# Matrix products that stream their columns by turns, and weight tiles that begin 64 bytes past a multiple of 256

## The chip, the cores and the metric

The kernel runs on one core of a Trainium2 chip, as one launch. The metric is the device time of the launch in microseconds (us): 1811.39 us is the median of 3 runs of the kernel before (1809.56 to 1812.52).

## The reference

Two blocks of layers on one sequence of 512 tokens with 1024 features, all in float32. Nearly all the arithmetic is in matrix products with weights that are read once from HBM:

```python
def reference(x, ...):
    # first block: width 1024, causal convolution of 31 taps, pooling, SwiGLU with 2816 hidden columns
    z = rmsnorm(x, g_mix) @ w_in + b_in
    y = concatenate([conv_group(z[..., :512], z[..., 512:1024]), pool_group(z[..., 1024:])])
    h = x + y @ w_out
    h = h + (silu(rmsnorm(h, g_ffn) @ w_gate) * (rmsnorm(h, g_ffn) @ w_up)) @ w_down
    x = rmsnorm(h, g_final)
    # second block: layer 0 gated causal attention (16 heads), layer 1 differential attention (8 heads)
    for layer in range(2):
        x = layer_norm(ALPHA * x + attention(x), ...)
        u = causal_conv3(x @ ffn_w_in[layer])          # 1024 -> 2 * 2816
        x = layer_norm(ALPHA * x + (silu(u[..., :2816]) * u[..., 2816:]) @ ffn_w_out[layer], ...)
```

## The kernel before

Activations lie with the features over the 128 partitions and the 512 tokens along the free dimension: XH and XL are [128, 8, 512], 2048 bytes for one row k of 128 features. The stationary operand of a product is a 128x128 piece of a weight matrix, the moving operand is such a row of activations (128x512), and the sum over k builds up in one bank of PSUM (bank0, bank1, and in places the banks called attended, score and turned).

TensorE takes float32 in a rounded form, so each operand is split in two: a top part (WH, XH, and HH and OH for the hidden columns and the attention's output) and a low part (WL, XL, HL, OL), the rest. One product is three matmuls, `product` at L982 to L985: WH with XL, WH with XH, WL with XH. Each matmul brings its own load of 128x128 weights (PEld in the profile, over the time of the matmul before).

A weight matrix is worked off in items, pieces of up to 8 rows k by 128 columns. SyncE fetches an item into `raw` (2 places), ScalarE writes its top part into WH (L1605), GpSimd the low part into WL (L742), 4 places each. The order of the items is fixed (the table STAGES). `step` (L987) waits for the halves of the item on w_lo and issues `product`, `item` loops over k, `whole` (L1011) is one item of 8 rows into one bank: 24 matmuls of 512 columns. VectorE or ScalarE reads the finished bank and gives it back over bank_read.

Some products don't run over 512 columns at once: `half_item` (L1036) and `stage_in_halves` (L1048) take 256 columns, so that the norm of one half of the tokens can be made beside the products of the other. `first_items`, `conv_low`, `mixer_items` and `last_rows_of` issue the same three matmuls in another order than `product`, since their operands become ready one row after the other. `conv_pairs` (L1284) runs a quarter of the convolution on TensorE, with diagonal matrices (dg_h, dg_l) as weights and u_h, u_l as moving operand, 256 columns, which begin 4 bytes later from one step m to the next. The two attention stages (qkv1, qkv2) weave: between the products of one pair of heads stand scores, transposes (`turn_map`, L1424) and value products of the pair before. These attention matmuls (`score_packed`, `score`, `attend_folded`, transposes) call pe.matmul directly; only `attend` of the second attention layer uses `product`.

Where the tiles lie in a partition matters for this change: XH, XL, raw, WH, WL, HH, HL, OH, OL, dg_h, dg_l, the value tiles and the identity all begin at a multiple of 256 bytes. u_h and u_l are the exception, since they are shifted. Rows of 2048 bytes and weight pieces of 512 bytes keep that, so in the kernel before the moving operand and the next weights both begin at a multiple of 256 (but for the convolution).

Of the kernel before, what the change touches and what calls it, by code (L numbers as in the profile page):

```python
# [61 lines left out]
RAW = 2  # L62
SLOTS = 4
HALF = S // 2
LAST_DOWN = (3, 3, 8, 8)
assert sum(LAST_DOWN) == FT

# [130 lines left out]
def two_blocks(nc, A, out):  # L198
    ctx = ExitStack()
    with ctx:  # L200
# [19 lines left out]
        yout = sb("yout", [P, 2 * QT, S])  # L220
        last_rows = sb("last_rows", [P, DT, S])
        raw = sb("raw", [P, RAW, DT, P])
        WH = sb("WH", [P, SLOTS, DT, P], F32R)
        WL = sb("WL", [P, SLOTS, DT, P], F32R)
        par = sb("par", [P, 6 * P])
# [2 lines left out]
        ident = identr.bitcast(F32)  # L228
        masks = sb("masks", [P, 2, P], F32R)
        work = sb("work", [P, 6, S])  # L230
        small = sb("small", [P, 108 + 20])

        tmp = [work[:, 0, :], work[:, 1, :]]
        ring = [work[:, i, :] for i in (0, 1, 4, 5)]
# [744 lines left out]

        @block.tensor  # L980
        def _(pe):
            def product(out_, wh, wl, xh, xl, start, stop):  # L982
                pe.matmul(out_, wh, xl, start=start, stop=False)  # L983
                pe.matmul(out_, wh, xh, start=False, stop=False)  # L984
                return pe.matmul(out_, wl, xh, start=False, stop=stop)  # L985

            def step(g, b, hi, lo, k0, k, kt, start, stop, turned=False):  # L987

# [57 lines left out]
            def stage_in_halves(name, m):  # L1046


                g, u = STAGES[name]
                for h in range(2):  # L1050
                    c = slice(h * HALF, (h + 1) * HALF)

                    def by_low(k):
                        pe.wait_ge(x_lo, DT + half_tile(m, h, k) + 1)
                        for j in range(2):
                            mm = pe.matmul(bank[(u + j) % 2][:, c], WH[:, (g + j) % SLOTS, k, :], XL[:, k, c],  # L1056
                                           start=False, stop=k == DT - 1)
                            if h == 1 and k == DT - 1:
                                mm.then_inc(item_done, 1)

                    for k in range(DT):
                        pe.wait_ge(x_top, half_tile(m, h, k) + 1)
                        for j in range(2):
                            if h == 0 and k == 0:
                                bank_free(Nth(u + j))
                                pe.wait_ge(w_lo, 2 * (g + j + 1))
                            s = (g + j) % SLOTS
                            pe.matmul(bank[(u + j) % 2][:, c], WH[:, s, k, :], XH[:, k, c], start=k == 0, stop=False)  # L1068
                            pe.matmul(bank[(u + j) % 2][:, c], WL[:, s, k, :], XH[:, k, c], start=False, stop=False)  # L1069
                        if k:  # L1070
                            by_low(k - 1)
                        if h == 0 and k == 2:
                            whole_sums(m, 1)
                        if h == 0 and k == 3:
                            half_stats(m, 1)
                        if h == 0 and k == 5:
                            half_widen(m, 1)
                    by_low(DT - 1)
# [167 lines left out]
            def first_items():  # L1246

                def by_low(k):
                    pe.wait_ge(x_lo, k + 1)
                    for j in range(2):  # L1250
                        mm = pe.matmul(bank[j][:, :], WH[:, j, k, :], XL[:, k, :], start=False, stop=k == DT - 1)
                        if k == DT - 1:
                            mm.then_inc(item_done, 1)

                for k in range(DT):
                    first_ready(k)
                    pe.wait_ge(x_hi, k + 1)
                    for j in range(2):
# [2 lines left out]
                            pe.wait_ge(w_hi, j + 1)  # L1261
                        elif k == DT // 2:
                            pe.wait_ge(w_lo, j + 3)
                        pe.matmul(bank[j][:, :], WH[:, j, k, :], XH[:, k, :], start=k == 0, stop=False)
                        if k == 0:
                            pe.wait_ge(w_lo, j + 1)
                        pe.matmul(bank[j][:, :], WL[:, j, k, :], XH[:, k, :], start=False, stop=False)
                    if k:
                        by_low(k - 1)
                by_low(DT - 1)  # L1270
# [33 lines left out]
            def mixer_items():  # L1304
# [13 lines left out]
                def conv_low(k):  # L1318
                    pe.wait_ge(cv_lo, k + 1)
                    for j in range(2):  # L1320
                        mm = pe.matmul(bank[(u + j) % 2][:, :], WH[:, (g + j) % SLOTS, k, :], XL[:, k, :], start=False, stop=k == CT - 1)
                        if k == CT - 1:
                            mm.then_inc(item_done, 1)

# [17 lines left out]
                for k in range(CT):  # L1342
                    pe.wait_ge(cv_hi, k + 1)
                    for j in range(2):
                        s = (g + j) % SLOTS
                        pe.matmul(bank[(u + j) % 2][:, :], WH[:, s, k, :], XH[:, k, :], start=False, stop=False)
                        pe.matmul(bank[(u + j) % 2][:, :], WL[:, s, k, :], XH[:, k, :], start=False, stop=False)
                    if k:
                        conv_low(k - 1)
                conv_low(CT - 1)  # L1350
# [109 lines left out]
            def last_rows_of(name, hi, hi_count, lo, lo_count):  # L1460
# [2 lines left out]
                pe.wait_ge(hi, hi_count)  # L1463
                for j in range(2):
                    s = (g + j) % SLOTS
                    pe.matmul(bank[j][:, :], WH[:, s, k, :], OH[:, k, :], start=False, stop=False)
                    pe.matmul(bank[j][:, :], WL[:, s, k, :], OH[:, k, :], start=False, stop=False)
                pe.wait_ge(lo, lo_count)
                for j in range(2):
                    pe.matmul(bank[j][:, :], WH[:, (g + j) % SLOTS, k, :], OL[:, k, :], start=False, stop=True).then_inc(item_done, 1)  # L1470

            def out_steps(name, ready, pairs, scored):

# [1210 lines left out]
```

## Time and profile before

| | before |
|---|---|
| median of 3 runs | 1811.39 us (1809.56 to 1812.52) |
| the profiled execution: time | 1808.84 us |
| the profiled execution: span, first to last instruction | 1807.0 us |
| TensorE matmuls | 8755, busy 98% of the span |
| TensorE weight loads | 8755, busy 82% |
| GpSimd, ScalarE, VectorE busy | 57%, 44%, 42% |
| HBM traffic over the span | 85 GB/s |
| granted TensorE clock, mean | 0.994 |

The span is 1.8 us shorter than the time of the same execution, and that execution is 2.6 us below the median. Matmuls are pipelined: the distance from one start to the next is what a matmul costs in a row of them, and not its own duration, which has its latency in it. So the busy share of PE says only that matmuls never stood still for long; how fast they went must be read from starts, or from a count in a stretch.

### The profile page before, as it was taken

To read this page: it belongs to the slowest core of one execution; us is meant where nothing else is said; L and a number is where in the kernel's file an instruction comes from. 1 tells how busy PE (TensorE), PEld (TensorE's weight loads), DVE (VectorE), ACT (ScalarE), POOL (GpSimd) and SP (SyncE) were. 2 spreads that over 40 slices of the span, in tenths; PEclk is the share of its full clock that TensorE was granted. 3 is DMA by queue.
4 is the path that set the end of the run, shared out by engine and by line. 5 is a ranking of instruction groups with operands and counts; after the bars stand their busy time and mean duration, and the time that the engine had idled before them with its cause. 6 is when DMAs were issued, how large, how long until landed. Compare 5 with 4: busy or idle time off the path is not lost.

```text
span 1807.0 us, 26859 instructions
## 1 busy us (share of the span) xinstructions
PE 1762.7 (98%) x8755; PEld 1476.5 (82%) x8755; DVE 765.9 (42%) x1382; ACT 796.0 (44%) x1674; POOL 1032.3 (57%) x926
## 2 busy tenths in 40 slices
PE   8999999999999999999999999999999999999997
PEld 6879888888887888788888888877777888888887
DVE  7973000001235556553333322487875533333224
ACT  5644332322245555464444422555565644444231
POOL 6966555555562333466666665655554666666651
PEclk9999999999999999999999999999999999999999
DMA  4312333333334454223333233333332233332332
GB/s 153 94 47 82 105 93 93 93 88 109 94 89 115 126 134 120 85 75 100 103 94 93 82 110 88 82 93 78 86 82 71 72 110 97 93 101 82 105 91 98
DMA packets 327252, 171.94 MB, mean 95 GB/s; under 512 B 43458, under 2 KB 316948, under 8 KB 327188
## 3 DMA queue, kind: packets, MB, share of 16 engines
q1 hardware_dynamic: 327172, 171.12, 33.7%
q8 instruction: 35, 0.57, 0.1%
q14 instruction: 29, 0.24, 0.0%
q10 hardware_dynamic: 16, 0.00, 0.0%
HBM read 152.15 MB, written 2.10 MB: 85 GB/s over the span
## 4 chain that ended last, share of the span: by engine, by line
PE 86%; DVE 9%; ACT 2%; issue 1%; POOL 1%; DMA 0%; DVEq 0%; SPq 0%; ACTq 0%
PE bank L983 24%; PE bank L985 23%; PE bank L984 23%; DVE score L2266 3%; PE attended L983 2%; PE attended L984 2%; PE attended L985 2%; PE turned L1424 1%; PE attended L1440 1%; PE bank L1056 1%; PE bank L1068 1%; DVE xres L2165 1%; PE bank L1069 0%; PE score L1417 0%; PE score L1407 0%
## 5 line engine op out<-in xcount | busy, mean ns | idle before, releaser
L742 POOL TENSOR_TENSOR WL<-raw,WH 128x512 fp32r<-128x512 f32 (+3 forms) x656 | 777.6, 1207 | 539.8 <-ACT WH L1605 537.2
L983 PE MATMUL bank<-XL,WH 128*128 128x512 f32 x1432 | 568.5, 397 | 3.7 <-DVE work L2577 1.2
L985 PE MATMUL bank<-XH,WL 128*128 128x512 f32 x1432 | 557.9, 390 | 0.0
L984 PE MATMUL bank<-XH,WH 128*128 128x512 f32 x1432 | 557.3, 389 | 0.0
L1605 ACT ACTIVATE WH<-raw 128x512 fp32r<-128x512 f32 (+3 forms) x656 | 338.4, 566 | 293.2 <-PE bank L985 186.5
L985 PEld LDWEIGHTS bank<-XH,WL 128*128 128x128 f32 x1432 | 269.4, 188 | 56.9
L983 PEld LDWEIGHTS bank<-XL,WH 128*128 128x128 f32 x1432 | 269.7, 188 | 55.9 <-DVE work L2577 1.5
L984 PEld LDWEIGHTS bank<-XH,WH 128*128 128x128 f32 x1432 | 269.9, 188 | 50.3
L983 PE MATMUL bank<-HL,WH 128*128 128x512 f32 (+1 forms) x528 | 198.6, 376 | 0.0
L985 PE MATMUL bank<-HH,WL 128*128 128x512 f32 (+1 forms) x528 | 198.4, 376 | 0.0
L984 PE MATMUL bank<-HH,WH 128*128 128x512 f32 (+1 forms) x528 | 198.4, 376 | 0.0
L869 POOL TENSOR_TENSOR HL<-hid,HH 128x512 f32 x66 | 85.1, 1290 | 70.7 <-ACT HH L1821 70.7
L2366 DVE SCALAR_TENSOR_TENSOR xres<-xres,bank 128x512 f32 (+1 forms) x27 | 18.6, 687 | 250.7 <-PE bank L985 247.9
L985 PEld LDWEIGHTS bank<-HH,WL 128*128 128x128 f32 x528 | 99.3, 188 | 18.2
L983 PEld LDWEIGHTS bank<-HL,WH 128*128 128x128 f32 x528 | 99.4, 188 | 18.0
L984 PEld LDWEIGHTS bank<-HH,WH 128*128 128x128 f32 x528 | 99.4, 188 | 17.9
L1861 ACT ACTIVATE pmap<-score,small 128x128 f32<-128x128 f32 (+3 forms) x128 | 67.3, 526 | 104.8 <-DVE small L2454 104.4
L2428 DVE TENSOR_TENSOR hid<-bank,act_g 128x512 f32<-128x512 f32 x21 | 14.5, 692 | 207.5 <-PE bank L985 203.9
L1959 ACT ACTIVATE hid<-bank,par 128x512 f32<-128x512 f32 x42 | 32.7, 778 | 143.5 <-PE bank L985 143.5
L2514 DVE SCALAR_TENSOR_TENSOR hid<-bank,par,hid 128x511 f32<-128x511 f32 x42 | 31.5, 749 | 150.7 <-ACT hid L1959 150.5
L2514 DVE SCALAR_TENSOR_TENSOR act_g<-bank,par,act_g 128x511 f32<-128x511 f32 x42 | 31.5, 750 | 133.8 <-ACT act_g L1959 133.8
L2454 DVE TENSOR_REDUCE small<-score 128x1 f32<-128x128 f32 (+3 forms) x128 | 62.1, 486 | 36.1 <-PE score L1409 23.7
(366 smaller groups left out, 2524.9 us busy)
## 6 DMA issues: line engine op xcount, KB each, us to landing
raw<-in_ffn_w_in SPq DMA_DIRECT2D x88, 512.0 KB, 3.7
raw<-in_w_gate SPq DMA_DIRECT2D x22, 512.0 KB, 3.6
raw<-in_w_up SPq DMA_DIRECT2D x22, 512.0 KB, 3.7
raw<-in_ffn_w_out SPq DMA_DIRECT2D x28, 384.0 KB, 3.2
raw<-in_ffn_w_out SPq DMA_DIRECT2D x28, 320.0 KB, 3.2
raw<-in_a_w_in SPq DMA_DIRECT2D x16, 512.0 KB, 3.9
raw<-in_kv_w SPq DMA_DIRECT2D x32, 256.0 KB, 3.0
raw<-in_w_in SPq DMA_DIRECT2D x12, 512.0 KB, 3.7
```

Source lines behind the costliest of these rows:

```text
L742: pool.tensor_tensor(wl, x, wh, ALU.subtract).then_inc(w_lo, 1)
L869: pool.tensor_tensor(HL[:, bass.ds(it * 2 + j, 1), :], hid[:, j:j + 1, :], HH[:, bass.ds(it * 2 + j, 1), :].bitcast(F32), ALU.subtract).th ...
L983: pe.matmul(out_, wh, xl, start=start, stop=False)
L984: pe.matmul(out_, wh, xh, start=False, stop=False)
L985: return pe.matmul(out_, wl, xh, start=False, stop=stop)
L1605: act.activation(wh, x, ACT.Copy).then_inc(w_hi, 1)
L1861: act.activation(pmap[:, n % 4, 0:k], sc[c][:, 0:k], ACT.Exp, bias=small[:, n % 4:n % 4 + 1], accum_out=small[:, 4 + n % 4:5 + n % 4]).the ...
L1959: act.activation(dst[:, j, :], ff_banks(it, j)[side][:, :], ACT.Identity, bias=ff_par(layer - 1, 3, n), scale=ff_par(layer - 1, 2, n)).the ...
L2266: ins = dve.scalar_tensor_tensor(out=vconv[:, c, :] if j == TAPS - 2 else part, in0=upad[:, c, j:j + S], scalar=tap(j, c), in1=part, op0=A ...
L2366: dve.scalar_tensor_tensor(out=r, in0=r, scalar=factor, in1=src[j][:, :].rearrange("p (a s) -> p a s", a=1), op0=ALU.mult, op1=ALU.add).th ...
L2454: dve.tensor_reduce(small[:, n % 4:n % 4 + 1], sc[c][:, 0:(n // 2 + 1) * P], AX_X, ALU.max, negate=True).then_inc(mx[c], 1)
L2514: own.link(dve.scalar_tensor_tensor(out=dst[:, j, 1:], in0=src[:, 0:S - 1], scalar=ff_par(layer - 1, 1, n), in1=dst[:, j, 1:], op0=ALU.mul ...
```

## The change

Each matmul of `product`, and of the functions that issue the same three, reads its moving operand in another order: 16 columns (64 bytes) of the first half of the row, then 16 of the second half, then the next 16 of the first, and so on. The output is written in the same order, so that each column lands where it did. With 512 columns the halves are 1024 bytes apart, with 256 columns 512 bytes. The second part is a tile of 64 bytes that nothing uses, odd_line, ahead of WH: WH and WL then begin 64 bytes past a multiple of 256, and so do par, ones, identr, masks and work, which lie behind them. `small` is 64 bytes smaller, so all that lies behind it (the hidden tiles, the attention's, the convolution's) stays where it was. The order of the instructions on all engines is the same as before, and their number too; only the access patterns of TensorE's moving operands and outputs, and addresses, differ.

Not changed are scores, transposes, `attend_folded`, `mixed` and the sums over partitions. In `attend`, `head_gates` and `conv_pairs` the columns go by turns, while their weights stay at multiples of 256.

```diff
@@ -62,6 +62,7 @@
 HALF = S // 2
+LINE = 16
@@ -220,6 +221,7 @@
         raw = sb("raw", [P, RAW, DT, P])
+        odd_line = sb("odd_line", [P, LINE])
         WH = sb("WH", [P, SLOTS, DT, P], F32R)
         WL = sb("WL", [P, SLOTS, DT, P], F32R)
...
-        small = sb("small", [P, 108 + 20])
+        small = sb("small", [P, 108 + 4])
@@ -979,10 +981,18 @@
         @block.tensor
         def _(pe):
+            def by_turns(x):
+
+                return x.rearrange("p (h l c) -> p l h c", h=2, c=LINE)
+
+            def times(out_, w, x, start, stop):
+
+                return pe.matmul(by_turns(out_), w, by_turns(x), start=start, stop=stop)
+
             def product(out_, wh, wl, xh, xl, start, stop):
-                pe.matmul(out_, wh, xl, start=start, stop=False)
-                pe.matmul(out_, wh, xh, start=False, stop=False)
-                return pe.matmul(out_, wl, xh, start=False, stop=stop)
+                times(out_, wh, xl, start, False)
+                times(out_, wh, xh, False, False)
+                return times(out_, wl, xh, False, stop)
@@ -1065,8 +1075,8 @@
                             s = (g + j) % SLOTS
-                            pe.matmul(bank[(u + j) % 2][:, c], WH[:, s, k, :], XH[:, k, c], start=k == 0, stop=False)
-                            pe.matmul(bank[(u + j) % 2][:, c], WL[:, s, k, :], XH[:, k, c], start=False, stop=False)
+                            times(bank[(u + j) % 2][:, c], WH[:, s, k, :], XH[:, k, c], k == 0, False)
+                            times(bank[(u + j) % 2][:, c], WL[:, s, k, :], XH[:, k, c], False, False)
...
```

The other places (`first_items`, `conv_low`, `mixer_items`, `last_rows_of`) are rewritten in the same way.

## Rows read from the trace of the kernel before

**Rows 1.** The page: busy time by engine, and the chain that ended last
```profile
PE 1762.7 (98%) x8755; PEld 1476.5 (82%) x8755; DVE 765.9 (42%) x1382; ACT 796.0 (44%) x1674; POOL 1032.3 (57%) x926
...
PE 86%; DVE 9%; ACT 2%; issue 1%; POOL 1%; DMA 0%; DVEq 0%; SPq 0%; ACTq 0%
```

**Rows 2.** Window: length; PE, PEld, DVE, ACT, POOL busy us (x instructions); clock, DMA
```profile
200.00:400.00 200.00, 200.00 (x884) 165.62 (x883) 13.14 (x19) 60.64 (x110) 114.54 (x92) 1.00 0.32 94
```

**Rows 3.** Timeline of matmuls, products of 512 columns: start and duration in us
```profile
299.65 0.39 PE L985 MATMUL bank<-XH,WL 128*128 128x512 f32 x1
299.88 0.39 PE L983 MATMUL bank<-XL,WH 128*128 128x512 f32 x1
...
301.46 0.39 PE L984 MATMUL bank<-XH,WH 128*128 128x512 f32 x1
```

**Rows 4.** Timeline of matmuls, products of 256 columns
```profile
1438.13 0.28 PE L1068 MATMUL bank<-XH,WH 128*128 128x256 f32 x1
...
1438.61 0.28 PE L1068 MATMUL bank<-XH,WH 128*128 128x256 f32 x1
```

**Rows 5.** Timeline of weight loads, in the stretch of rows 3
```profile
299.88 0.19 PEld L984 LDWEIGHTS bank<-XH,WH 128*128 128x128 f32 x1
```

**Rows 6.** Chain in order of time: four transposes of 128 columns
```profile
1228.62 0.44 PE turned L1424 x4
```

**Rows 7.** Timeline of matmuls, first attention, products behind matmuls of 128 columns
```profile
593.49 0.39 PE L984 MATMUL bank<-XH,WH 128*128 128x512 f32 x1
593.72 0.39 PE L985 MATMUL bank<-XH,WL 128*128 128x512 f32 x1
593.96 0.40 PE L983 MATMUL bank<-XL,WH 128*128 128x512 f32 x1
...
595.34 0.39 PE L983 MATMUL bank<-XL,WH 128*128 128x512 f32 x1
595.56 0.39 PE L984 MATMUL bank<-XH,WH 128*128 128x512 f32 x1
```

**Rows 8.** Timeline of matmuls, convolution, operand 4 bytes later each step
```profile
86.50 0.29 PE L984 MATMUL attended<-u_h,dg_h 128*128 128x256 f32 x1
86.62 0.29 PE L985 MATMUL attended<-u_h,dg_l 128*128 128x256 f32 x1
...
87.22 0.28 PE L984 MATMUL attended<-u_h,dg_h 128*128 128x256 f32 x1
87.33 0.28 PE L985 MATMUL attended<-u_h,dg_l 128*128 128x256 f32 x1
```

**Rows 9.** Groups from 100 us on, by form: count, busy us, mean ns, idle
```profile
L983 PE MATMUL bank<-XL,WH 128*128 128x512 f32 x1335 | 532.3, 399 | 3.1 <-DVE work L2577 1.2 <-DVE VX L2465 0.7 <-DVE xres L2366 0.7
...
L983 PE MATMUL bank<-HL,WH 128*128 128x512 f32 x462 | 179.8, 389 | 0.0
L1068 PE MATMUL bank<-XH,WH 128*128 128x256 f32 x160 | 44.9, 304 | 4.5 <-ACT XH L1658 4.3
L1424 PE MATMUL turned<-identr,pmap 128*128 128x128 f32 x240 | 43.8, 281 | 11.3 <-DVE pmap L2612 9.3 <-DVE pmap L2483 1.9
...
L983 PE MATMUL bank<-OL,WH 128*128 128x512 f32 x62 | 25.7, 414 | 0.8 <-POOL WL L742 0.8
...
L983 PE MATMUL attended<-XL,WH 128*128 128x512 f32 x64 | 25.0, 390 | 0.0
...
L983 PE MATMUL attended<-HL,WH 128*128 128x256 f32 x66 | 19.4, 294 | 0.0
L983 PE MATMUL bank<-HL,WH 128*128 128x256 f32 x66 | 18.8, 285 | 0.0
```

**Rows 10.** Chain in order of time, between 33 and 95 us
```profile
33.74 8.00 DVE score L2266 x13
...
84.06 11.20 DVE score L2266 x17
```

**Rows 11.** Groups on GpSimd, 200 to 400 us
```profile
L742 POOL TENSOR_TENSOR WL<-raw,WH 128x512 fp32r<-128x512 f32 x73 | 92.6, 1290 | 20.0 <-ACT WH L1605 20.0
L869 POOL TENSOR_TENSOR HL<-hid,HH 128x512 f32 x19 | 24.5, 1291 | 65.4 <-ACT HH L1821 65.4
```

More of the change, by code:

```diff
@@ L1250, in by_low @@
                     for j in range(2):
-                        mm = pe.matmul(bank[j][:, :], WH[:, j, k, :], XL[:, k, :], start=False, stop=k == DT - 1)
+                        mm = times(bank[j][:, :], WH[:, j, k, :], XL[:, k, :], False, k == DT - 1)
                         if k == DT - 1:
@@ L1263, in first_items @@
                             pe.wait_ge(w_lo, j + 3)
-                        pe.matmul(bank[j][:, :], WH[:, j, k, :], XH[:, k, :], start=k == 0, stop=False)
+                        times(bank[j][:, :], WH[:, j, k, :], XH[:, k, :], k == 0, False)
                         if k == 0:
                             pe.wait_ge(w_lo, j + 1)
-                        pe.matmul(bank[j][:, :], WL[:, j, k, :], XH[:, k, :], start=False, stop=False)
+                        times(bank[j][:, :], WL[:, j, k, :], XH[:, k, :], False, False)
                     if k:
@@ L1320, in conv_low @@
                     for j in range(2):
-                        mm = pe.matmul(bank[(u + j) % 2][:, :], WH[:, (g + j) % SLOTS, k, :], XL[:, k, :], start=False, stop=k == CT - 1)
+                        mm = times(bank[(u + j) % 2][:, :], WH[:, (g + j) % SLOTS, k, :], XL[:, k, :], False, k == CT - 1)
                         if k == CT - 1:
@@ L1345, in mixer_items @@
                         s = (g + j) % SLOTS
-                        pe.matmul(bank[(u + j) % 2][:, :], WH[:, s, k, :], XH[:, k, :], start=False, stop=False)
-                        pe.matmul(bank[(u + j) % 2][:, :], WL[:, s, k, :], XH[:, k, :], start=False, stop=False)
+                        times(bank[(u + j) % 2][:, :], WH[:, s, k, :], XH[:, k, :], False, False)
+                        times(bank[(u + j) % 2][:, :], WL[:, s, k, :], XH[:, k, :], False, False)
                     if k:
@@ L1465, in last_rows_of @@
                     s = (g + j) % SLOTS
[L1466 to L1467 removed]
+                    times(bank[j][:, :], WH[:, s, k, :], OH[:, k, :], False, False)
+                    times(bank[j][:, :], WL[:, s, k, :], OH[:, k, :], False, False)
                 pe.wait_ge(lo, lo_count)
                 for j in range(2):
[L1470 removed]
+                    times(bank[j][:, :], WH[:, (g + j) % SLOTS, k, :], OL[:, k, :], False, True).then_inc(item_done, 1)
             def out_steps(name, ready, pairs, scored):
```

## The prediction

> **What bounds the kernel now.** I read the busy shares and the chain first. TensorE is busy for 98% of the span, and 86% of the chain that ended last lies on it; the other engines are at 42 to 57% [rows 1]. So what counts is the pace at which matmuls follow each other. That is read from starts, not from durations, which overlap. In the stretch from 200 to 400 us there are 884 matmuls in 200 us, 226 ns each, with the clock granted in full, which is its level of 2.4 GHz [rows 2]; the timeline gives the same, 1.81 us for the eight distances from 299.65 to 301.46 [rows 3]. At one column in a cycle 512 columns need 213.3 ns. So each matmul takes 13 ns more than its columns. In products of 256 columns four distances take 0.48 us, 120 ns each, against 106.7 ns of columns [rows 4]: again 13 ns. The excess does not grow with the columns; it comes once for each matmul, as the load of weights does.
>
> What is done once for each matmul: a load of 128 columns of weights, which starts as the matmul before it starts, at 299.88 both [rows 3, 5]. How long weights stream can be seen where the moving operand is short: four transposes of 128 columns take 0.44 us, 110 ns each, twice the 53 ns of their columns [rows 6]. That is 128 weights at half the pace, one in 0.83 ns. So in a product of 512 columns the weights of the next are read over the first half of the stream, and in one of 256 over nearly all of it.
>
> Does the excess come from the two reads meeting? Two rows speak for it. The same product in the same tiles takes 235 ns (593.49 to 593.96 is two distances) right behind the short matmuls of the attention and 220 to 230 ns some ten matmuls later, with no wait in between [rows 7]: what differs is when the load falls against the stream. And in the convolution, where the moving operand begins 4 bytes later each step, distances go between 0.11 and 0.12 us within the same run of products [rows 8]. A fixed cost of exchanging weights would show neither.
>
> **The change, part by part.** (1) The columns by turns. Now the moving stream covers addresses at twice the pace of the weights and overtakes them again and again. By turns it covers 64 bytes of one half and 64 of the other in the time in which the weights cover 64 bytes: both advance at one pace, modulo 256 bytes. (2) The 64 bytes ahead of WH set the weights one step of 64 bytes apart from the moving operand, which begins at a multiple of 256. If collisions go by address in steps of 64 bytes, repeated after 256, the two never meet. No row shows such a layout. As an estimate from the paces: if one read of weights in four hits the part that the moving stream is in, and each costs that stream one cycle, 128 / 4 x 0.417 ns = 13.3 ns, which is the excess as measured in rows 3 and 4.
>
> How much of the 13 ns goes? The bounds are 13 (all) and 0. The nearest row below full is the load itself, which takes 110 ns where 106.7 are streamed [rows 6]: some 2 to 3 ns for each instruction remain whatever is read. The load starts up to some ns behind the matmul, so at the beginning the two may touch. I take 9 ns, so 217 to 218 ns for 512 columns and 111 for 256; 11 ns is the good case, 5 the poor one.
>
> The Trainium skill (TensorE: Matmul & The Clock Gate, Wait — 56ns, not 53.3ns?) gives 512 columns / 2.4 GHz + about 2.5 ns for matmuls back to back, 215.8 ns; the trace has 226, so by that page 10 to 11 ns would be there to be had.
>
> The sum. Products on TensorE's path, from 100 us on: three matmuls each of 1335 (XL), 462 (HL), 62 (OL) and 64 (attended) with 512 columns, 5769 matmuls; three each of 160 and twice 66 with 256 columns, 876 [rows 9]. The first 100 us don't count: there the chain runs over VectorE's convolution [rows 10], and faster products in it only wait. Smaller groups (the out stages' last items) I leave out. 6645 x 9 ns = 60 us. Given back: in the stage in halves the products follow ScalarE, which writes XH (4.3 us of waits now), and in the second attention TensorE waits for VectorE's pmap, 9.3 us now [rows 9]; what gets faster ahead of such a wait makes it longer. Half of the gain there, 480 / 2 x 9 ns = 2 us, and some 3 us in the second attention, an estimate from eight units with 72 products each: 8 x 72 x 9 ns / 2. Sum: 60 - 5 = 55 us. The profiled execution takes 1808.8 us, so 1754; the median of the runs is 2.6 us over it, so about 1756.
>
> What could be late next elsewhere: an item of 24 matmuls lasts 5.4 us now and 5.2 then. GpSimd's two WL halves take 2.6 us of it, and it is idle for 85 us of this window waiting on ScalarE's WH and HH [rows 11]; ScalarE is busy for 61 of 200 us and the DMA engines for 0.32 [rows 2]. So all have cover. Not changed: 240 transposes and the other short matmuls, bound by their loads. The products whose weights stay at a multiple of 256 (`attend`, `head_gates`, `conv_pairs`) may stay as they are or lose some ns: some 120 on the path, at most 2 us. The shift of work and par moves no instruction and changes no size; I cost it at nothing, and were it a few ns for each of VectorE's and ScalarE's instructions, they are idle for over half of the span [rows 1].
>
> **The rivals.**
> (a) Nothing moves. The excess is the price of exchanging the weights, the paces of the reads don't matter, and the differences in rows 7 and 8 come from the short neighbours. For it: 226 and 120 ns are very steady, whatever the other engines do [rows 2 to 4]. Against it: rows 7 and 8. Time: 1811, within 4.
> A rule of the Trainium skill says the same (TensorE: Matmul & The Clock Gate, Step-by-step: what each phase is for): TensorE has two independent read ports, and loading the next weights takes no bandwidth from the running matmul. By it no gain is possible here.
> (b) Slower: the jumps cost. Each moving operand and each output now has 32 runs of 16 columns, so 31 jumps, with 512 columns. A jump that costs one cycle of 2.4 GHz, in the read or in the accumulating write, adds 31 x 0.417 = 13 ns to 5769 matmuls and 15 x 0.417 = 6 ns to 876: 80 us. All of it is on the path: 1891 without a gain, and some 1835 with the gain of part (1). It decides from 0.3 ns a jump on (9 / 31). No row has a moving operand with jumps. The range of the convolution's distances, 0.11 to 0.12, is from operands that begin off any line, and no start of that kind costs more than 10 ns there [rows 8]; that speaks against a large price of a single jump, not against a small one.
> The Trainium skill has a rule for this (PSUM — Partial Sum Buffer, Specifications (TRN2)): PSUM's cachelines are 8 bytes, and any access pattern that isn't contiguous slows matmuls significantly. Runs of 64 bytes keep every such line whole, so read closely it would not bind here; no row shows it.
> (c) The step of 64 bytes is the wrong one. At one pace, streams that collide stay together: then the load's whole 107 ns are affected instead of a quarter. The dearest distance in rows 7 is 8 to 9 ns over the usual; at that price 6645 x 9 ns = 60 us, 1871. For it: the load starts some ns late, toward the place where the moving stream comes. Against it: a stream that is stopped falls back, and then both are apart.
>
> **How the numbers follow.** Faster by 5 to 13 ns a matmul: chance 0.62, around 1756; 13 ns (90 us gross) would be 1726, 5 ns some 1783. A smaller gain, 1 to 5 ns: 0.08. No change (a): 0.10. Slower: (b) 0.14, (c) 0.06. The forecast is 1756. The range runs from 1728 (nearly all of the excess gone) over the small gains and no change up to 1835, the mild form of (b). A difference of under 0.2% is about what cannot be told from none here: faster 0.70, same 0.10, slower 0.20. The likeliest case has 1728 to 1785 as its own range.
>
> **What would show it.** Right: in the stretch from 200 us the count in 200 us rises from 884 to about 918 (200 / 0.218), the distances of 256-column products go from 120 to 111 ns, and the transposes stay at 110. The stages keep their order, and TensorE's waits for pmap grow a little. For (a) the count stays at 884. For (b) 512-column distances grow by twice what 256-column ones do, since the jumps are twice as many; for (c) both grow by the same. It would be wrong in size if WL or hid became TensorE's waits, or if the excess were cut to 216 ns, which would bring 1742.

## The result: 4.2% slower

| | before | after |
|---|---|---|
| median | 1810.47 us (1809.52 to 1812.52, 4 runs) | 1885.95 us (1883.23 to 1889.47, 4 runs) |
| ratio after / before | | 1.0416 (1.0392 to 1.0441) |
| the profiled execution: time, span | 1808.84, 1807.0 us | 1883.43, 1881.6 us |
| distance of matmuls, products of 512 columns, gate-and-up stages | 226.7 ns | 240.0 ns |
| the same, 256 columns | 120 ns | 120 ns |

The forecast was 1756, the range 1728 to 1835: the sign was wrong, and the time lies 51 us beyond the range. "Before" here is the median of four runs, one more than in the median that stands ahead.

The page of the changed kernel, against [rows 1]:

```profile
PE 1839.8 (98%) x8755; PEld 1497.4 (80%) x8755; DVE 771.5 (41%) x1382; ACT 797.9 (42%) x1674; POOL 1025.4 (54%) x926
...
PE 90%; DVE 5%; ACT 2%; issue 1%; POOL 1%; DMA 1%; SPq 0%; DVEq 0%; ACTq 0%
```

TensorE has grown by 77.1 us of busy time, the span by 74.6; the busy times of the other engines changed by 2 to 7 us. The window of [rows 2], with the same columns, and then the timeline of [rows 3]:

```profile
200.00:400.00 200.00, 200.00 (x835) 159.18 (x834) 11.77 (x17) 58.06 (x105) 109.53 (x88) 1.00 0.31 90
```

```profile
299.78 0.40 PE L990 MATMUL bank<-XL,WH 128*128 128x512 f32 x1
300.02 0.40 PE L990 MATMUL bank<-XH,WH 128*128 128x512 f32 x1
...
301.46 0.40 PE L990 MATMUL bank<-XH,WH 128*128 128x512 f32 x1
```

835 matmuls stand where there were 884: 240 ns each, with the clock granted in full in both. Seven distances take 1.68 us, and all are alike. TensorE's waits have hardly moved; the one that grew most, of the scores for ScalarE's pmap, went from 0.5 to 1.4 us. Its waits for single releasers (us in total, times, longest), against the idle times in [rows 9]:

```profile
PE turned L1434 <- DVE pmap L2622: 8.9, 8, 1.7
...
PE bank L990 <- ACT XH L1668: 4.2, 12, 0.7
```

Where the 74.6 us lie, by the time from a stage's first matmul to its last in the two traces:

| | before, us | after, us | more |
|---|---|---|---|
| up to the first gate-and-up stage | 169.3 | 173.1 | 3.8 |
| three gate-and-up stages, 1008 matmuls each | 3 x 228.3 | 3 x 241.7 | 40.2 |
| down stages, twice 462 and once 396 matmuls | 298.5 | 316.1 | 17.6 |
| first attention with its output and the halves | 301.4 | 307.1 | 5.7 |
| second attention, likewise | 303.1 | 309.7 | 6.6 |

That is 73.9 of 74.6 us, and nearly all of it in the products: 5769 matmuls of 512 columns, as the prediction counted them, by 13.3 ns is 77 us. In the attention stages less comes of it, since many products there stood at 231 to 236 ns already before, behind short matmuls [rows 7].

Two corrections to what stands ahead. The XL matmuls of `stage_in_halves` (L1056 before, L1066 after) do not go by turns; they are contiguous in both kernels. And the weights of `head_gates` have 16 columns, 64 bytes, for each row k, one row behind the other, so only every fourth piece of them begins at a multiple of 256 bytes, in both kernels.

### The profile page after: what moved, and what is told of

It reads as the page before. It is cut to its first block, busy times and chain, and to the rows that moved or that the text cites. A ratio compares the mean times of both kernels' runs of the same rounds, so it can differ in the third digit from the quotient of the medians.

```text
span 1881.6 us, 26859 instructions
## 1 busy us (share of the span) xinstructions
PE 1839.8 (98%) x8755; PEld 1497.4 (80%) x8755; DVE 771.5 (41%) x1382; ACT 797.9 (42%) x1674; POOL 1025.4 (54%) x926
## 4 chain that ended last, share of the span: by engine, by line
PE 90%; DVE 5%; ACT 2%; issue 1%; POOL 1%; DMA 1%; SPq 0%; DVEq 0%; ACTq 0%
PE bank L990 75%; PE attended L990 6%; PE turned L1434 1%; PE score L990 1%; PE attended L1450 1%; PE bank L1066 1%; DVE small L2619 1%; DVE xres L2175 0%; DVE small L2464 0%; ACT xres L1651 0%; PE score L1418 0%; PE score L1417 0%; PE score L1427 0%; ACT pmap L1871 0%; PE score L1426 0%
## 5 line engine op out<-in xcount | busy, mean ns | idle before, releaser
L990 PE MATMUL bank<-XH,WH 128*128 128x512 f32 (+1 forms) x1616 | 631.1, 393 | 8.0 <-ACT XH L1668 4.2
L990 PE MATMUL bank<-XH,WL 128*128 128x512 f32 (+1 forms) x1616 | 626.9, 390 | 0.2 <-POOL WL L744 0.2
L990 PE MATMUL bank<-XL,WH 128*128 128x512 f32 x1456 | 593.6, 409 | 3.5 <-DVE work L2587 1.1
L990 PEld LDWEIGHTS bank<-XH,WH 128*128 128x128 f32 x1616 | 309.0, 191 | 77.5 <-ACT XH L1668 8.5
L990 PEld LDWEIGHTS bank<-XH,WL 128*128 128x128 f32 x1616 | 308.9, 191 | 71.1 <-POOL WL L744 0.6
L990 PEld LDWEIGHTS bank<-XL,WH 128*128 128x128 f32 x1456 | 278.8, 192 | 68.8 <-DVE work L2587 1.4
L990 PE MATMUL bank<-HL,WH 128*128 128x512 f32 (+1 forms) x528 | 204.8, 388 | 0.0
L990 PE MATMUL bank<-HH,WL 128*128 128x512 f32 (+1 forms) x528 | 204.6, 387 | 0.0
L990 PE MATMUL bank<-HH,WH 128*128 128x512 f32 (+1 forms) x528 | 204.6, 387 | 0.0
```

The costliest lines, as they stand in the source:

```text
L990: return pe.matmul(by_turns(out_), w, by_turns(x), start=start, stop=stop)
```

## Experiments

All distances of 512-column matmuls below are means over a whole stage, from the starts in the trace; those of 256-column matmuls are means over stretches of 42 or 48 of them, waits left out. For orientation: the kernel before, contiguous and with the weights at a multiple of 256 bytes ("at 0"), has 226.7 ns for 512 columns and 120 for 256. The six stages that are used as separate trials are the three gate-and-up stages (they begin at about 170, 820 and 1470 us, by up to 30 us apart from kernel to kernel) and the three down stages behind them. Kernels that ran once have one time and no interval.

### Each part alone

**e1_turns_only**: the columns by turns, the weights at 0. Against the changed kernel:

```diff
-        odd_line = sb("odd_line", [P, LINE])
...
-        small = sb("small", [P, 108 + 4])
+        small = sb("small", [P, 108 + 20])
```

> Columns by turns, weight tiles back at a multiple of 256 bytes. Theory A (every jump of the moving stream or of its output costs, the place of the weights is nothing): as the changed kernel, 1886 us within 3, 512-column products 240 ns apart. Theory B (reads of weights and of moving columns collide by address, and the step of 64 bytes was put on the wrong side): products of 512 columns change their distance by more than 3 ns against 240, time away from 1886 by more than 20 us.

Measured: 1884.37 us, ratio 1.041 (1.0388 to 1.0432), 240.0 and 120 ns. That is the changed kernel's time, so the 64 bytes do nothing once the columns go by these turns, and the whole loss comes from the turns.

**e2_offset_only**: the weights 64 bytes past, the columns contiguous. Against the changed kernel:

```diff
-                return pe.matmul(by_turns(out_), w, by_turns(x), start=start, stop=stop)
+                return pe.matmul(out_, w, x, start=start, stop=stop)
```

> Weight tiles 64 bytes past a multiple of 256, columns in their own order as before. Theory A: as the kernel before, 1810 us within 3, distances of 227 and 120 ns. Theory B: distances move off 227 ns by some ns, in either direction, time off 1810 by more than 10 us.

Measured: 1838.89 us, ratio 1.0158 (1.0132 to 1.0185). The window of [rows 2] and the timeline:

```profile
200.00:400.00 200.00, 200.00 (x858) 161.13 (x858) 12.46 (x18) 59.61 (x108) 112.45 (x89) 1.00 0.31 92
```

```profile
300.16 0.40 PE L990 MATMUL bank<-XL,WH 128*128 128x512 f32 x1
300.39 0.39 PE L990 MATMUL bank<-XH,WH 128*128 128x512 f32 x1
300.62 0.40 PE L990 MATMUL bank<-XH,WL 128*128 128x512 f32 x1
300.86 0.39 PE L990 MATMUL bank<-XL,WH 128*128 128x512 f32 x1
```

233.3 ns, as 231 and 236 in turn, where there were 226.7, though no instruction or access pattern differs from the kernel before: only addresses. And in the products of 256 columns the sign is the other one: four of the six stretches of 42 or 48 such products are at 113.3 to 113.4 ns, the other two at 117.8, against 120. So where the weights lie matters by 2 to 7 ns, and the excess over the columns is no fixed price: it is 13.3 and 13 ns at 0, and at 64 it is 20 ns for 512 columns and 7 or 11 for 256.

### Is it the jumps?

**e3_runs**: the changed kernel with turns of another length in five of the stages.

```diff
+            order[:] = [(2, 32), (2, 32)]      # first gate-and-up stage
...
+            order[:] = [(2, 64), (2, 64)]      # first down stage
...
+            order[:] = [(2, 128), (2, 128)]    # second gate-and-up
...
+            order[:] = [(2, 8), (2, 8)]        # second down
...
+            order[:] = [(2, 4), (2, 4)]        # third gate-and-up
```

> By turns with another length of run in each feed-forward stage: 32 columns in the first gate-and-up stage, 64 in the first down stage, 128 in the second gate-and-up, 8 in the second down, 4 in the third gate-and-up, 16 elsewhere. Theory A (a price per jump of two column cycles, 0.83 ns, with the excess of the load gone): 512-column distances of 213.3 + 0.83 x runs: 227 ns at 32 columns (16 runs), 220 at 64, 217 at 128, 267 at 8, 320 at 4. Theory A' (half a ns per jump on top of the 227 of before): 233 at 32, 230 at 64, 228 at 128, 253 at 8. Theory B (pace against 64-byte banks): 64 and 128 columns give 227 as before, 32 something of its own.

The windows of these five stages, in this order:

```profile
200.00:400.00 200.00, 200.00 (x847) 159.72 (x846) 11.75 (x17) 57.89 (x105) 111.66 (x89) 1.00 0.31 91
415.00:515.00 100.00, 100.00 (x430) 80.60 (x429) 17.73 (x18) 23.00 (x54) 54.21 (x57) 1.00 0.33 96
850.00:1050.00 200.00, 200.00 (x859) 161.13 (x858) 65.65 (x90) 84.62 (x143) 123.23 (x90) 1.00 0.31 92
1065.00:1165.00 100.00, 100.00 (x413) 77.88 (x412) 22.78 (x24) 22.67 (x53) 51.89 (x54) 1.00 0.32 91
1500.00:1700.00 200.00, 200.00 (x794) 150.28 (x793) 60.49 (x82) 80.47 (x132) 113.80 (x84) 1.00 0.30 87
```

| columns in a run | 128 | 64 | 32 | 16 | 8 | 4 |
|---|---|---|---|---|---|---|
| jumps | 3 | 7 | 15 | 31 | 63 | 127 |
| ns, weights at 64 | 233.3 | 233.3 | 236.7 | 240.0 | 243.3 | 252.2 |

No price of a jump fits this. Seven jumps cost nothing over the contiguous 233.3 of e2; 31 cost 6.7 ns; 127, four times as many, cost 19 ns, less than three times as much. What is free is a run of 256 bytes or more. Theory A' expected 233 ns at 32 columns and 253 at 8, and measured were 236.7 and 243.3.

**e4_sides**: which side pays? The moving read by turns with the output contiguous in the first pair of gate-and-up and down stages; the output by turns with the read contiguous in the second pair; both in the third.

```diff
-                return pe.matmul(by_turns(out_), w, by_turns(x), start=start, stop=stop)
+                return pe.matmul(by_turns(out_, 0), w, by_turns(x, 1), start=start, stop=stop)
...
+            order[:] = [(1, 16), (2, 16)]
...
+            order[:] = [(2, 16), (1, 16)]
```

> First feed-forward pair of stages: only the moving operand is read by turns, the output is written in one run, so its columns land permuted; second pair: only the output is written by turns, from columns read in one run; third pair: both, as in the changed kernel. The output isn't the reference's. Theory R (the read pays for the jumps): 240 ns in the first pair, 227 in the second. Theory W (the accumulating write pays): 227 in the first, 240 in the second. If both sides pay in common, 233 in each.

```profile
200.00:400.00 200.00, 200.00 (x835) 159.18 (x834) 11.76 (x17) 57.90 (x105) 109.43 (x88) 1.00 0.31 91
850.00:1050.00 200.00, 200.00 (x859) 161.15 (x858) 65.05 (x89) 85.26 (x143) 122.51 (x90) 1.00 0.32 93
1500.00:1700.00 200.00, 200.00 (x835) 159.18 (x834) 64.19 (x87) 83.24 (x139) 118.64 (x87) 1.00 0.31 92
```

Read by turns 240, write by turns 233.3, both 240. The whole price is on the read; the write by turns, in runs of 64 bytes that lie 1024 bytes apart, costs nothing over e2. In the runs below read and write always go in the same order, and that the write is free in those other orders too was not measured.

The rule of the Trainium skill that any output pattern in PSUM that isn't contiguous slows matmuls (PSUM — Partial Sum Buffer, Specifications (TRN2)) is not borne out for such runs: 859 matmuls in 200 us with it against 858 without.

### Which orders of the read are dear?

**e5_orders_0**: the weights at 0, the two halves contiguous, and a different order of 16-column pieces in each stage. "Every n-th run" reads all runs that are n x 64 bytes apart, then goes back for the next ones.

```diff
+            order[0], wide[0] = ("p (l h c) -> p h l c", dict(h=2, c=16)), P   # every 2nd run
...
+            order[0], wide[0] = ("p (l h c) -> p h l c", dict(h=4, c=16)), P   # every 4th
...
+            order[0], wide[0] = ("p (l h c) -> p h l c", dict(h=8, c=16)), P   # every 8th
...
+            order[0], wide[0] = ("p (h l c) -> p l h c", dict(h=4, c=16)), P   # out of 4 quarters
...
+            order[0], wide[0] = ("p (h l c) -> p l h c", dict(h=2, c=64)), P   # turns of 64
```

> Weights at a multiple of 256 bytes; products of 512 columns read and write their 32 runs of 16 columns in another order in each feed-forward stage, all else contiguous: first gate-and-up, every second run (128 bytes on, then back for the others); first down, every fourth (256 bytes on); second gate-and-up, every eighth (512 bytes on); second down, by turns out of four quarters; third gate-and-up, by turns as in the changed kernel; third down, by turns with 64 columns. Theory S (the read pays when runs that follow each other lie in the same 64 bytes of 256): 227 ns for every second run and for turns of 64, 240 for the turns of the change, more than 240 for every fourth, every eighth and four quarters, some 13 ns more for each doubling of the repeats, up to 253. Theory J (each jump pays, whatever its distance, and the 8 jumps of 64-column turns are too few to see): all orders with runs of 16 at 240, turns of 64 at 230.

The windows of the first four stages:

```profile
200.00:400.00 200.00, 200.00 (x835) 156.97 (x834) 12.45 (x18) 56.72 (x103) 107.64 (x86) 1.00 0.31 91
415.00:515.00 100.00, 100.00 (x420) 79.18 (x419) 18.28 (x18) 22.48 (x52) 51.48 (x55) 1.00 0.33 96
850.00:1050.00 200.00, 200.00 (x867) 162.68 (x866) 66.40 (x90) 86.25 (x144) 123.13 (x92) 1.00 0.32 93
1060.00:1160.00 100.00, 100.00 (x434) 81.36 (x433) 23.51 (x24) 24.03 (x56) 54.11 (x56) 1.00 0.34 99
```

**e6_orders_64** is the same with the weights 64 bytes past, and **e10_distances** has six more orders with the weights at 0.

```diff
# e6_orders_64, against e5_orders_0
+        odd_line = sb("odd_line", [P, LINE])
...
# e10_distances, stage by stage
+            order[0], wide[0] = ("p (h l c) -> p l h c", dict(h=8, c=16)), P
...
+            order[0], wide[0] = ("p (h l c) -> p l h c", dict(h=16, c=16)), P
...
+            order[0], wide[0] = ("p (h l c) -> p l h c", dict(h=4, c=32)), P
...
+            order[0], wide[0] = ("p (h l c) -> p l h c", dict(h=8, c=32)), P
...
+            order[0], wide[0] = ("p (h l c) -> p l h c", dict(h=4, c=64)), P
...
+            order[0], wide[0] = ("p (h l c) -> p l h c", dict(h=2, c=32)), P
```

> The same orders with the weights 64 bytes past a multiple of 256. If the two reads meet by address (L), orders whose distance differs from the kernel with weights at a multiple of 256 are those that depend on it: contiguous and 64-column turns 233 against 227, the change's turns 240 in both. Theory S alone: each order as in the other kernel, but for the 6 ns of the contiguous ones. Theory J: 240 for all with runs of 16.

> Weights at a multiple of 256; 512-column products by turns out of 8 parts (256 bytes apart) with runs of 16 in the first gate-and-up stage, out of 16 parts (128 bytes apart) in the first down, out of 4 parts with runs of 32 in the second gate-and-up, out of 8 with runs of 32 in the second down, out of 4 with runs of 64 in the third gate-and-up, out of 2 with runs of 32 in the third down. If the distance of the jumps sets the price (512 bytes cheap at 231 ns, 1024 and 128 dear at 240): 239, 240, 229, 235, 227 and 233 in this order. If the length of the runs alone did: all runs of 16 at 240, all of 32 at 233, 64 at 227; the 231 of the four quarters speaks against that already.

Two windows of e10_distances, 4 parts by 32 columns and 4 parts by 64:

```profile
850.00:1050.00 200.00, 200.00 (x859) 160.91 (x858) 66.06 (x90) 85.51 (x143) 121.20 (x90) 1.00 0.32 93
1500.00:1690.00 190.00, 190.00 (x840) 157.34 (x839) 64.10 (x87) 82.82 (x139) 119.04 (x87) 1.00 0.33 96
```

All orders in one table, ns per matmul of 512 columns; the distance is that between the starts of successive runs:

| columns in a run | distance, bytes | weights at 0 | at 64 |
|---|---|---|---|
| contiguous | | 226.7 | 233.3 |
| 64 | 1024 (the changed kernel's halves) | 226.7 | 233.3 |
| 64 | 512 | 226.7 | |
| 32 | 1024 | 236.7 | 236.7 |
| 32 | 256 | 236.7 | |
| 32 | 512 | 233.3 | |
| 16 | 1024 (the changed kernel) | 240.0 | 240.0 |
| 16 | 512, every 8th run | 231.1 | 236.7 |
| 16 | 512, out of 4 quarters | 231.1 | 236.7 |
| 16 | 256, every 4th run | 239.5 | 237.3 |
| 16 | 256, out of 8 parts | 239.5 | |
| 16 | 128, every 2nd run | 240.0 | 242.2 |
| 16 | 128, out of 16 parts | 240.0 | |

Two theories fall here: that each jump costs the same (all 16-column orders have about 31, and they range from 231.1 to 240), and that it is dear to read the same 64 of 256 bytes several times in a row. "Every 8th" does that for four runs and is cheap; "every 2nd" never does it and is dear. What holds in all rows: runs of 256 bytes in order are free. Of the others, with the weights at 0, steps of 512 bytes cost 4.4 ns with 16 columns, and steps of 128, 256 or 1024 cost 13. Shorter is not always dearer: at steps of 512 bytes 32 columns cost 6.6 ns and 16 columns 4.4. With the weights at 64 the same steps cost 3.4 (512), 4.0 (256), 6.7 (1024) and 8.9 ns (128) over the contiguous 233.3. e10's six results came in about the order expected from e5, but the 32-column ones were 2 to 4 ns dearer, and two of them, expected at 233 and 235, came out alike.

### Is it the load of the weights?

**e7_widths**: the weights at 0; each load inside a sum has only 64 or 16 of the 128 columns, contiguous in the first pair of stages and by turns in the second.

```diff
+                n = wide[0] if w.shape[-1] == P and x.shape[-1] == S and not start and not stop else w.shape[-1]
+                return pe.matmul(by_order(out_)[0:n], w[:, 0:n], by_order(x), start=start, stop=stop)
```

> Weights at a multiple of 256, contiguous columns; in the first gate-and-up stage the products of 512 columns take 64 weight columns, in the first down stage 16 (but for the first and the last matmul of a sum), in the second pair the same two widths with columns by turns; the rest of each weight piece is left out, so the output isn't the reference's. Theory L (the excess is made while weights are read): 227 falls to about 220 with 64 and to 215 to 217 with 16 weight columns, and 240 falls in the same way. Against L (the head gates of the kernel before, with 16 weight columns, are 229 to 235 ns apart): 227 and 240 stay within 5 ns.

Contiguous with 64, contiguous with 16, by turns with 64, by turns with 16:

```profile
200.00:390.00 190.00, 190.00 (x828) 114.55 (x827) 12.46 (x18) 57.76 (x105) 108.50 (x86) 1.00 0.33 95
400.00:500.00 100.00, 100.00 (x433) 42.19 (x432) 17.90 (x18) 24.39 (x57) 54.95 (x57) 1.00 0.33 96
850.00:1040.00 190.00, 190.00 (x793) 112.56 (x792) 60.52 (x83) 78.95 (x132) 111.94 (x83) 1.00 0.31 90
1050.00:1150.00 100.00, 100.00 (x418) 41.89 (x417) 24.21 (x27) 24.33 (x56) 54.79 (x55) 1.00 0.31 91
```

229.7, 231.7, 240.0 and 240.0 ns. The load engine's time has fallen to 42 of 100 us in the stages with 16 columns, and the matmuls are not a nanosecond faster; contiguous, they are 3 to 5 ns slower. This is the run that decides most: the excess is not made by the length of time in which weights are read. It doesn't say that the loads have no part in it: each matmul still brings one, and no run here leaves the loads out, so a price for each load, whatever its width, was not tested.

The trace of before pointed the same way, in rows that I had not read. `head_gates` uses weights of 16 columns; timeline of before, matmuls and then their loads:

```profile
532.43 0.40 PE L983 MATMUL attended<-XL,PTH 128*16 128x512 f32 x1
532.67 0.39 PE L984 MATMUL attended<-XH,PTH 128*16 128x512 f32 x1
...
533.59 0.39 PE L985 MATMUL attended<-XH,PTL 128*16 128x512 f32 x1
```

```profile
532.67 0.10 PEld L985 LDWEIGHTS attended<-XH,PTL 128*16 128x16 f32 x1
532.90 0.09 PEld L983 LDWEIGHTS attended<-XL,PTH 128*16 128x16 f32 x1
```

Five distances in 1.16 us, 232 ns each, beside loads of 0.10 us instead of 0.19 [rows 5]. Two things differ there from the products at 226.7 ns, the width of the load and its place, which moves on by 64 bytes with each row k; so these rows agree with e7 but would not decide alone.

### Where the tiles lie

**e8_x_at_128** puts XH, XL and raw at 128 bytes past a multiple of 256 and leaves the weights at 0; **e9_w_at_192** puts the weights at 192; **e11_wl_alone** leaves WH at 0 and puts WL at 64, and with it par and work behind it. All are contiguous.

```diff
# e8_x_at_128
-        to_line = sb("to_line", [P, 32])      # ahead of XH, XL and raw
...
+        to_line = sb("to_line", [P, 32])      # behind them
# e9_w_at_192
+        small = sb("small", [P, 108 + 4])     # ahead of WH
# e11_wl_alone
         WH = sb("WH", [P, SLOTS, DT, P], F32R)
+        odd_line = sb("odd_line", [P, LINE])
         WL = sb("WL", [P, SLOTS, DT, P], F32R)
```

> Columns contiguous; XH, XL and raw begin 128 bytes past a multiple of 256, WH and WL and the hidden tiles at one. The gate-and-up stages then have weights and moving operand 128 bytes apart, the down stages are as before. Theory L: gate-and-up products move off 227 ns by several ns (64 bytes apart gave 233), down products stay at 227. If only the moving operand's own place counts, gate-and-up moves and weights play no part: told apart by the kernel with the weights alone moved (233 for both kinds). If neither: 227 in both, 1810 us.

> Columns contiguous, weights 192 bytes past a multiple of 256 (small lies ahead of them). 512-column products were 226.7 ns apart with weights at 0, 233.3 with 64, 256-column ones 120 and 113.5. If the place of the weights sets a state of the two reads, 192 gives a third pair of numbers, between 220 and 240 and between 110 and 122. If 0 is a special place and all others are alike: 233 and 113.5, 1839 us.

> Columns contiguous; WH at a multiple of 256, only WL (and par, work behind it) 64 bytes past one. If each load's own place sets the distance of the matmul beside it: the matmul beside WL's load (XH with WH) at 233, the other two at 227, mean 229, about 1818 us. If the places of par and work (ScalarE and VectorE) made the 233 of the offset kernel and not the weights: 233 for all three, 1839 us. If neither: 227 and 1811 us.

The window 200 to 400 us of the three, one fence each:

```profile
200.00:400.00 200.00, 200.00 (x859) 160.93 (x858) 12.45 (x18) 59.58 (x108) 112.54 (x90) 1.00 0.31 91
```

```profile
200.00:400.00 200.00, 200.00 (x876) 164.09 (x875) 13.15 (x19) 60.80 (x111) 115.33 (x91) 1.00 0.32 93
```

```profile
200.00:400.00 200.00, 200.00 (x868) 162.53 (x867) 12.46 (x18) 59.60 (x108) 113.93 (x90) 1.00 0.32 92
```

| XH, XL at | weights at | 512 columns, ns | 256 columns, ns | run, us |
|---|---|---|---|---|
| 0 | 0 (before) | 226.7 | 120 | 1810.47 |
| 0 | 64 (e2) | 233.3 | 113.3 or 117.8 | 1838.89 |
| 0 | 192 (e9) | 228.9 | 113.3 or 117.8 | 1815.42 |
| 0 | WH 0, WL 64 (e11) | 231.1 | 117.8 | 1830.84 |
| 128 | 0 (e8) | 232.4 to 233.3 | 120 | 1829.64 |

In e8 the down stages, whose moving operands are the hidden tiles at 0, stay at 226.7 ns within the same run, and only the products with XH and XL are slow. So the place of the weights counts (e2, e9) and that of the moving operand too (e8). The table fits the theory that only the distance between the two counts, modulo 256; but no run moves both together, so that is not shown.

For 256 columns the placement alone doesn't fix the distance. In e9 the same 48 matmuls, of HH and HL with WH and WL, are 113.3 ns apart at the end of the first down stage and 117.8 ns at the end of the second. Ten distances of each:

```profile
508.13 0.28 PE L996 MATMUL bank<-HL,WH 128*128 128x256 f32 x1
...
509.26 0.28 PE L996 MATMUL bank<-HH,WH 128*128 128x256 f32 x1
```

```profile
1145.94 0.28 PE L996 MATMUL bank<-HL,WH 128*128 128x256 f32 x1
...
1147.12 0.28 PE L996 MATMUL bank<-HH,WH 128*128 128x256 f32 x1
```

Both paces are steady, and what settles which of them a stretch takes stays open.

e11 was to say which load it is that costs. If it were the load of WL beside the matmul XH with WH, that one distance should be dear; I measured 229.1 there, and 235.9 for the matmul after it, XH with WL, beside the load of the next WH at 0. So a misplaced load is paid later than where it lies, or by the matmul that uses it; this run can't tell which. It also can't tell the place of WL from that of par and work; that these alone don't make e2's 233.3 follows from the 231.1 here.

A rule of the Trainium skill (TensorE: Matmul & The Clock Gate, Step-by-step: what each phase is for) has the weights and the moving operand on two independent read ports, so that a load takes nothing from the running matmul. It doesn't hold to the nanosecond here: addresses alone, of weights or of moving operand, raise the distance by 2 to 7 ns in four layouts. It is right on the larger point that my prediction denied: a load that reads for less time makes no matmul faster (e7).

### A run with jumps that cost nothing

**e12_turns_of_64**: the changed kernel with turns of 64 columns instead of 16, and the weights at 0.

```diff
-LINE = 16
+LINE = 64
...
-        odd_line = sb("odd_line", [P, LINE])
...
-        small = sb("small", [P, 108 + 4])
+        small = sb("small", [P, 108 + 20])
```

> The changed kernel with runs of 64 columns (256 bytes) in place of 16 in all products, and with the weights back at a multiple of 256. If the order of the 64-byte pieces within 256 bytes is what the read pays for, and jumps as such are free: 227 ns and 120 ns everywhere, the time of the kernel before, 1811 us within 3. If a jump has a price of its own (7 a matmul with 512 columns): over 1811 by 5868 x 7 x the price, 17 us at one column cycle.

```profile
200.00:400.00 200.00, 200.00 (x884) 165.58 (x884) 13.14 (x19) 59.83 (x109) 115.06 (x92) 1.00 0.33 95
```

Measured: 1811.06 us, ratio 1.0001 (0.999 to 1.0012), 226.7 and 120 ns. 884 matmuls in 200 us, the number of [rows 2]. An order with seven jumps in each operand and output is as good as none, over the whole kernel. No kernel of this study is faster than the one before.

## Why the prediction was wrong

**What bounds the kernel** held. TensorE is the bound before and after, and the distance of its matmuls is the whole difference: by 13.3 ns 77 us, of 75 measured.

**"Does the excess come from the two reads meeting?"** is the step that failed: it took the 13 ns for a collision with the load, which a new order of the columns would remove, and so put the columns by turns at a gain of 9 ns a matmul. They cost 13.3 ns instead (e1), and the cost is that of reading the moving operand in these runs of 64 bytes (e4). The step before it, "it comes once for each matmul, as the load of weights does", prepared the failure. I had two sizes of product, both with 13 ns over their columns, and read a price per matmul from them. Both were taken at one placement of the tiles. With the weights at 64 the same two sizes have 20 ns, and 7 or 11. And by turns the excess is not alike for the sizes: 240.0 - 213.3 = 26.7 ns for 512, 120 - 106.7 = 13.3 for 256, and in `attend`, where 24 matmuls have 384 columns, about 180 - 160 = 20 (177 to 183). That would be 0.83 ns for each run of 16 columns in all three, but it is no rule: the halves lie 1024, 512 and 768 bytes apart, and at 512 columns the distance of the runs alone makes 231.1 or 240.0 ns (e5). That 256 columns stayed at 120 ns fits the low price of steps of 512 bytes; no other step was tried with 256 columns. From a price per matmul I went on to the load as its cause; e7 takes away half and seven eighths of the load and the price stays.

**"By turns both advance at one pace"** was worth nothing: 240.0 ns with the weights at 0 (e1) and at 64 alike, and with 16 weight columns alike. That both streams advance at one pace is itself worked out from the access patterns, and no trace shows it. So the term 9 ns x 6645 had the wrong sign for 5769 matmuls (+13.3 in place of -9) and was zero for 876. The good case has a slip in its working: 13 ns by 6645 are 86 us gross, and not 90.

**The two rows that I took as support** did not carry it. The 235 ns behind short matmuls [rows 7] differ from 227 by something that stays open; what they show is that 13 ns is not fixed. That a fixed price was wrong was right; that the load was what varies did not follow. The convolution [rows 8] showed starts off a line at no price. By turns the same products pay for it; timeline after, where the operand begins 4 bytes later every three matmuls:

```profile
87.20 0.28 PE L990 MATMUL attended<-u_h,dg_h 128*128 128x256 f32 x1
87.33 0.28 PE L990 MATMUL attended<-u_h,dg_l 128*128 128x256 f32 x1
87.45 0.31 PE L990 MATMUL attended<-u_l,dg_h 128*128 128x256 f32 x1
...
87.73 0.32 PE L990 MATMUL attended<-u_h,dg_l 128*128 128x256 f32 x1
87.88 0.32 PE L990 MATMUL attended<-u_l,dg_h 128*128 128x256 f32 x1
88.03 0.32 PE L990 MATMUL attended<-u_h,dg_h 128*128 128x256 f32 x1
```

0.12 to 0.13 us apart where the runs begin at a multiple of 16 bytes, 0.15 at 4, 8 and 12 bytes past one, some 25 ns more for 16 runs. Nearly all of this lies beside VectorE's convolution. "The first 100 us don't count" was right but for 2.2 us: the first product behind the convolution starts at 112.6 us in place of 110.4, and the time up to the first gate-and-up stage grows by 3.8 us in all.

The Trainium skill gives SBUF lines of 16 bytes and a penalty for each crossing to a new one (SBUF — State Buffer, Specifications (TRN2)). The starts that are dear are those that split a line at both ends of each run, so the trace agrees in kind; contiguous, the same crossings cost nothing that could be seen.

**The rivals.** (b) named the right sign and nearly the right time: 1891 without a gain, against 1885.95. Its size of 13 ns per 512 columns is the measured one, and its mechanism is not. By its own sign, 512-column distances should grow by twice what 256-column ones do; they grew by 13.3 and 0. That sign could not decide, since the two sizes jump by different steps, 1024 and 512 bytes; the runs with other orders do. Its write half is free (e4), jumps after 256 bytes are free (e3, e12), and about 31 jumps of 512 bytes cost a third of 31 jumps of 1024. The upper end of the range failed with it: it was taken from (b)'s mild form, with part (1)'s gain in it, so that both ends rested on the same untested gain. With 1891 as that end the range would have held. (c) foretold the same growth in both sizes, and a dependence on the 64 bytes: neither came. (a) foretold no change, on the ground that reads don't disturb each other: wrong here too, though e12 shows how near its number an order can stay.

**Smaller steps.** The waits for pmap and XH stayed (8.9 and 4.2 us). The `attend` and `head_gates` products of 512 columns, costed at "may lose some ns", went to 240 ns as all others. Nothing else became late: WL and the hidden tiles have more cover at 240 ns than at 227.

**What stays open.** What makes four successive pieces of 64 bytes cheap and steps of 512 bytes nearly so; whether any of the excess is a price for each load; why 226.7 and not 213.3 is the floor of all that was tried with 512 columns; and how the placement of the weights acts, since the length of the load is not what counts, and why the same layout has two paces at 256 columns. Many of the mean distances (226.7, 233.3, 236.7, 240.0, 243.3) are within 0.1 ns of whole multiples of 3.33 ns, eight cycles at 2.4 GHz, others (231.1, 237.3, 252.2) are not; I have no explanation for that which a run has tested.

## What to carry to other kernels

Let the moving operand of a matmul read whole 256 bytes in order: runs of 16 columns cost up to 13 ns for each matmul of 512 columns and runs of 4 columns 19 (with the weights at 64), while runs of 64 columns or more were free, and so was an output by turns in runs of 64 bytes. Where TensorE is the bound, measure the placement of its tiles modulo 256 bytes, for each size of product by itself: the same shift cost 6.6 ns at 512 columns and gained 2 to 7 at 256. And before a cause is taken from a number that two rows share, look in the trace for a row in which that cause is smaller: here 16-column weights stood in it, at 232 ns.

## What the hardware showed that I had not expected

- An order of reading that touches the same bytes costs between 0 and 19 ns for 512 columns over the contiguous one, and the distance between its runs counts: with 16 columns in a run 512 bytes have 231.1 ns, and 128, 256 or 1024 bytes 239.5 to 240.0.
- Moving the weights and the tiles behind them by 64 bytes, with no other change, makes the kernel 1.6% slower (e2), and moving them by 192 costs 2.2 ns a matmul (e9).
- At 256 columns one layout has two steady paces: 113.3 ns in some stretches and 117.8 in others, for the same products (e9).
- Smaller weight loads make matmuls of contiguous columns slightly slower and not faster: 226.7 ns with 128 columns, 229.7 with 64, 231.7 with 16 (e7).
- By turns of 16 columns out of two halves the excess is 13.3, 20 and 26.7 ns at 256, 384 and 512 columns, with the halves 512, 768 and 1024 bytes apart, while contiguous reads with the weights at 0 have 13.3 ns at 256 and at 512.
